# Attention: GpSimd pre-adds the sums of one step in nine (j = 4) in place of two (j = 2 and j = 6)

## The reference

```python
s = jnp.einsum('bqhgd,bkhd->bhgqk', qi, k)     # qi already scaled by Dh ** -0.5
p = jax.nn.softmax(s, axis=-1)
return jnp.einsum('bhgqk,bkhd->bqhgd', p, v)
```

## Time and profile before

| | |
|---|---|
| median of 3 runs | 3883.38 us (3882.13 to 3886.03) |
| the profiled execution | 3884.3 us |
| its span in the profile | 3882.8 us |
| attention stage | about 385 to 1220 us |
| TensorE / VectorE / ScalarE / GpSimd busy, whole span | 91% / 50% / 41% / 27% |

### The profile page before, as it was taken

One profiled execution on the slowest core, in us unless ns is written; L12 is line 12 of the kernel. 1 busy time (PEld: TensorE's weight loads), 2 busy tenths in 40 slices (PEclk: granted clock), 3 DMA queues, 4 the chain that ended last, 5 costly groups with the idle time before them and its releaser, 6 DMA issues. The chain is left out here.

```text
span 3882.8 us, 49412 instructions
## 1 busy us (share of the span) xinstructions
PE 3544.4 (91%) x17922; PEld 2928.6 (75%) x17922; DVE 1958.2 (50%) x2948; ACT 1583.5 (41%) x2216; POOL 1047.6 (27%) x606
## 2 busy tenths in 40 slices
PE   5886999999996999687869799999999999999998
PEld 2764777777775999466758588888888888888897
DVE  2775899999984111345833333343334333433354
ACT  2442888888885111573224422222222222222233
POOL 0553999999993000011201100000000000000000
PEclk8997999999997999667989899999999999999999
DMA  4332111111102221224545643343334333433374
GB/s 165 104 118 83 39 44 44 44 43 44 44 23 90 83 80 65 84 88 125 155 141 173 200 123 97 114 150 97 96 118 141 97 107 103 147 94 101 108 206 152
DMA packets 375237, 400.99 MB, mean 103 GB/s; under 512 B 37588, under 2 KB 282548, under 8 KB 375092
## 3 DMA queue, kind: packets, MB, share of 16 engines
q1 hardware_dynamic: 358888, 358.26, 29.6%
q0 software_dynamic: 8432, 31.46, 2.2%
q10 hardware_dynamic: 7776, 9.44, 0.7%
HBM read 318.02 MB, written 81.08 MB: 103 GB/s over the span
## 5 line engine op out<-in xcount | busy, mean ns | idle before, releaser
L798 POOL TENSOR_TENSOR att_tlo<-att_prob,att_thi 128x1024 fp32r<-128x1024 f32 x292 | 693.5, 2400 | 78.0 <-ACT att_thi L967 78.0
L1989 ACT ACTIVATE ff_whi<-ff_ws 128x2048 fp32r<-128x2048 f32 (+1 forms) x170 | 317.5, 1867 | 901.6 <-PE ff_p L333 883.9
L331 PE MATMUL ff_p<-ff_hhi,ff_whi 128*128 128x512 f32 (+1 forms) x1760 | 650.5, 370 | 35.5 <-DVE ff_hlo L2045 22.7
L332 PE MATMUL ff_p<-ff_hlo,ff_whi 128*128 128x512 f32 (+1 forms) x1760 | 649.5, 369 | 0.0
L333 PE MATMUL ff_p<-ff_hhi,ff_wlo 128*128 128x512 f32 (+1 forms) x1760 | 649.5, 369 | 0.0
L1993 DVE TENSOR_TENSOR ff_wlo<-ff_ws,ff_whi 128x2048 fp32r<-128x2048 f32 (+1 forms) x170 | 378.4, 2226 | 386.9 <-ACT ff_whi L1989 386.7
L1935 POOL TENSOR_TENSOR ff_rs<-ff_ms,neg_half 128x1 f32<-128x1 f32 x18 | 9.9, 552 | 1596.0 <-DVE ff_ms L2065 1596.0
L331 PEld LDWEIGHTS ff_p<-ff_hhi,ff_whi 128*128 128x128 f32 x1760 | 333.6, 190 | 93.1 <-issue 37.9
L962 ACT ACTIVATE att_prob<-att_p_s 128x512 f32<-128x512 f32 x584 | 341.1, 592 | 103.2 <-PE att_p_s L858 95.6
L333 PEld LDWEIGHTS ff_p<-ff_hhi,ff_wlo 128*128 128x128 f32 x1760 | 333.5, 189 | 55.5
L332 PEld LDWEIGHTS ff_p<-ff_hlo,ff_whi 128*128 128x128 f32 x1760 | 333.7, 190 | 54.8
(11 more groups left out here) (242 smaller groups left out, 6200.8 us busy)
## 6 DMA issues: line engine op xcount, KB each, us to landing
ff_ws<-in_w_ffn_dram SPq DMA_DIRECT2D x320, 512.0 KB, 4.7
att_aw<-in_ada_w_dram SPq DMA_DIRECT2D x8, 2048.0 KB, 8.4
proj_d<-gp_out SPq DMA_DIRECT2D x18, 784.0 KB, 4.0
hT_d<-qkv_hT SPq DMA_DIRECT2D x18, 512.0 KB, 2.8
qT_d<-qkv_qT SPq DMA_DIRECT2D x18, 512.0 KB, 2.8
att_qa<-qT_d SPq DMA_DIRECT2D x36, 256.0 KB, 2.8
gp_h<-hT_d SPq DMA_DIRECT2D x18, 512.0 KB, 4.9
qkT_d<-gs_qkT SPq DMA_DIRECT2D x18, 512.0 KB, 2.9
```

The source lines that it names most:

```text
L331: pe.matmul(out, ah, bh, start=first, stop=False)
L332: pe.matmul(out, ah, bl, start=False, stop=False)
L798: pool.tensor_tensor(tlo[:, sl, :], prob[:, sl, :], thi[:, sl, :].bitcast(F32), ALU.subtract).then_inc(s.lo, 1)
L1989: act.activation(whi[:, par, 0:cols], ws[:, par, 0:cols], ACT.Copy).then_inc(s.w_hi, 1)
```

## The change

One line: `FOLDED` names step 4 in place of steps 2 and 6. GpSimd's pre-adds of steps 2 and 6 go, and it pre-adds step 4. VectorE adds the two halves of steps 2 and 6 itself, and takes one pre-added tile for step 4. `ADDS` becomes 17 in place of 16, the buffer `fold` has one row in place of two.

```diff
     PLAN = [3, 2, 1, 2, 2, 3, 3, 0, 0]
     PLAN_FIRST = [3, 2, 1, 2, 2, 3, 3, 2, 0]
     AHEAD = 2
-    FOLDED = (2, 6)
+    FOLDED = (4,)
     BANKS = 3
     ADDS = 2 * NS - len(FOLDED)
```

## The result

The changed kernel takes 3890.4 us at the median (20 runs) against 3883.4 us for the kernel before (20 runs). The ratio is 1.0021, with a 95% interval of 1.0014 to 1.0028: slower by 8.2 us by the ratio and 7.0 by the medians, with 5.4 and 10.9 as the interval's ends. The profiled execution took 3894.1 us, with a span of 3892.6, 9.8 more than before. The two medians stand 7.0 apart, the two profiled executions 9.8; the difference between these is what single executions scatter by.

The account below looks back on a forecast made before the run. The prediction took a TensorE-VectorE loop over a ring of two maxima banks as the bound. Its terms, 15 x 0.53 + 15 x 0.12 - 0.5 - 0.9 = +8.4 us, gave a median of 3891.8 us, range 3883.5 to 3898.5.

Parts of the forecast that it names:

- Step 1: GpSimd in each latent unit: losing one pre-add of two, 1.29 us, gains nothing in units 1 to 30.
- Step 2: VectorE: one more add per unit; the one in kernel step 7 costs nothing, output product 0.12 late.
- Step 3: TensorE: a later reduce delays the 11th maxima product from 2.34 to 2.61, and the second exponential to 3.62.
- Step 4: Kernel step 5: VectorE idles 0.40 for GpSimd's pre-add, so TensorE issues the 15th product 0.53 later, at 6.95.
- Step 5: Rest of the unit: the 0.53 us stays in units with a chunk; units without one keep +0.12.
- Step 6: Ends of the stage: -0.5 us in unit 0 and -0.9 in the last latent unit, as waits for pre-adds go.
- Absorbed: Rival: existing waits or a shorter wait in kernel step 5 take the shift; 3882 to 3885 us, chance 0.23.
- No give-back: Rival: units without a chunk also keep 0.53; +14.5 us, 3897.9; chance 0.15 together with VectorE-bound.
- VectorE-bound: Rival: VectorE binds throughout, each extra add costs 0.60 in 31 units; +18.6 us, 3902; chance 0.15 shared with No give-back.
- GpSimd binds: Rival: each unit shortens by up to 1.25 us; 3845 us, or 3863 with half lost to VectorE; chance 0.08.
- The fold runs early enough: Rival: kernel step 4's exponentials don't move and VectorE comes later than 5.62; same time as Absorbed, no chance of its own.

Follow-up runs that it names:

- e3: The change with no pre-adds on GpSimd, so VectorE makes 18 adds per unit: 3883.2 us, ratio 1.0001 to the kernel before.
- e1: The change with GpSimd pre-adding step 2 alone in place of step 4: 3881.0 us, ratio 0.9994 to the kernel before.
- e2: The change with GpSimd pre-adding step 6 alone in place of step 4: 3883.8 us, ratio 1.0003 to the kernel before.
- e4: The change, with VectorE's first reduce in step 5 made before the pre-added sum: 3877.3 us, ratio 0.9984 to the kernel before.
- e9: GpSimd pre-adds steps 2 and 4, against 2 and 6 in the kernel before; VectorE still makes 16 adds: 3900.8 us, ratio 1.0047.
- e10: Pre-adds of steps 2 and 4 as in e9, plus step 5's first reduce before the pre-added sum: 3872.7 us, ratio 0.9971 to the kernel before.
- e7: The change with the modulation chunk's products behind step 6 in place of step 5: 3891.3 us, ratio 1.0019 to the kernel before.
- e8: The kernel before with the modulation chunk's products behind step 6 in place of step 5: 3890.1 us, ratio 1.0016.
- e6: The change with GpSimd pre-adding steps 2, 4 and 6 in place of 4 alone: 3904.5 us, ratio 1.0054 to the kernel before.
- e11: The change with the first reduce ahead of the add in steps 3 and 5: 3869.9 us, ratio 0.9966 to the kernel before.
- e5: The kernel before, with VectorE's first reduce in step 5 made before its two adds: 3883.6 us, ratio 0.9998.

## Why the prediction was right, and where it was not

*Step 1 (GpSimd's relief is worth nothing)* held. e3 takes all pre-adds away and no unit is shorter for it. The rule of the Trainium skill ("Perfetto Trace Analysis", Identifying the Most-Contended Engine) to optimise the engine with the highest busy share first failed here: GpSimd went from 96% to 90% of the stretch and the time rose. In e3 it went to 86% and the time stayed.

*Step 2 (the extra adds)* held to 0.01 us: the one in step 7 is free (e1), the one in step 3 moves the output product by 0.11 (2.47 for 2.48 predicted).

*Step 3 (a later reduce in step 3 holds TensorE)* held: the 11th product at 2.60 for 2.61, the exponential at 3.60 for 3.62. Alone it costs 0.10 to 0.12 per unit (e2, e3), so in units with a chunk it is a part of the 0.53 and the wait itself is the other 0.43.

*Step 4 (the new wait)* held in place and size: pre-add at 4.28 (4.29), add at 5.61 (5.62), reduce at 6.22 (6.22), 15th product at 6.95 (6.95). The waits sum to 10.2 us in 30 units (0.40 each predicted, 0.34 by the trace's count). GpSimd was free in front of the pre-add, as said. e4, e9 and e10 show that the loss is this wait with a reduce behind it: longer wait, larger loss; reduce moved ahead, no loss.

*Step 5 (what becomes of 0.53)* held: 0.53 in units with a chunk, 0.12 in the others; 9.7 us over 29 units and 9.8 with unit 30's own, where the sum had 9.75 over 30. e7 and e8 show the reason given for the difference. What the prediction didn't see is that step 3's late reduce alone gives the same 0.12 in units without a chunk (e2).

*Step 6 (the ends of the stage)* failed: predicted -0.5 and -0.9, measured 0.0 and +0.6. At the reciprocal of unit 1 the change is 0.11 late (423.14 against 423.03), but it entered the stage 0.10 late. From unit 30's reciprocal to the last one it takes 72.91 us against 72.24; 0.11 of these 0.67 are unit 30's own. In unit 0 the gain was there (the chunk's products began at 403.02 in place of 403.49), and was lost in step 7. Not all of it was the pre-add's: the granted clock is 0.78 and 0.88 from 395 to 400 and 400 to 405 us in the kernel before, and 1.00 in the change. Unit 0 has two maxima products there (`PLAN_FIRST`), so that VectorE's extra add stands between two reduces and not in front of an idle. VectorE's timeline of unit 0 in the change:

```profile
401.26 0.70 DVE L1037 TENSOR_TENSOR att_p_sum<-att_p_sum,att_fold 128x512 f32<-128x512 f32 x1 [1.47 <-POOL att_fold L796]
...
408.05 0.69 DVE L1037 TENSOR_TENSOR att_p_sum<-att_p_sum,att_prob 128x512 f32<-128x512 f32 x1
408.65 0.68 DVE L1013 TENSOR_REDUCE att_mx<-att_p_r 128x2 f32<-128x512 f32 x1
409.25 0.69 DVE L1037 TENSOR_TENSOR att_p_sum<-att_p_sum,att_prob 128x512 f32<-128x512 f32 x1
409.85 0.68 DVE L1013 TENSOR_REDUCE att_mx<-att_p_r 128x2 f32<-128x512 f32 x1
```

and in the kernel before:

```profile
408.54 0.69 DVE L1037 TENSOR_TENSOR att_p_sum<-att_p_sum,att_fold 128x512 f32<-128x512 f32 x1
409.14 1.29 DVE L1013 TENSOR_REDUCE att_mx<-att_p_r 128x2 f32<-128x512 f32 x2
```

Three instructions before, four after. I had taken the plan of the other units for unit 0 too.

In the last latent unit the VectorE wait of 3.7 us went, as predicted (one of 1.8 for the pre-add of step 4 came), but TensorE's clock fell at other places. Windows of the change (clock is the third number from the end), then of the kernel before at the same places of the unit:

```profile
1178.00:1188.00 10.00, 7.81 (x29) 6.33 (x29) 6.53 (x12) 7.69 (x13) 8.95 (x5) 0.83 0.04 14
1188.00:1196.00 8.00, 6.74 (x35) 5.20 (x35) 4.87 (x8) 7.16 (x11) 8.00 (x4) 1.00 0.15 49
...
1200.00:1210.00 10.00, 7.71 (x34) 6.02 (x32) 4.51 (x9) 6.85 (x12) 4.75 (x2) 0.83 0.00 0
```

```profile
1168.00:1178.00 10.00, 7.81 (x35) 6.24 (x35) 6.05 (x11) 8.90 (x15) 10.00 (x5) 1.00 0.04 13
1178.00:1186.00 8.00, 5.66 (x24) 4.39 (x23) 4.67 (x8) 5.50 (x9) 8.00 (x5) 0.80 0.14 49
...
1190.00:1200.00 10.00, 7.24 (x39) 5.68 (x37) 5.06 (x10) 8.17 (x14) 5.19 (x3) 1.00 0.01 2
```

TensorE idled 2.6 us for the spread reciprocals in both. In the change the granted clock is 0.83 in the mean of that stretch: a matmul of 512 columns takes 0.63 us up to 4.7 us after the unit's reciprocal, where it takes 0.39 in the kernel before, so this part ran at the lower level, 1.2 GHz. It makes ScalarE's second exponential of step 4 1.02 us later after the reciprocal than before (1182.65 - 1178.58 against 1171.73 - 1168.68).

That is not the loss at the end yet. The kernel before has such a stretch later, from 14.5 to 17.5 us after its reciprocal (0.80 in the mean of the window), and at VectorE's first copy of a context unit's sum (line 1034) that follows it the change is 0.99 us ahead (21.31 against 22.30 after the reciprocal). The predicted gain stood there, with the clock's part in it. Then the change has a second stretch at the lower level, from 25.8 to 28.4 (the window of 0.83 from 1200 us), where the kernel before has 1.00, and the next reciprocal comes at 31.80 against 31.23. So it is where these stretches fell that made the term positive.

That the same idle doesn't always end in a drop makes this term one that I could not have predicted from the rows; the range of -1.25 to 0 should have allowed for it. No experiment was made to settle when it drops, so this stays open, and so does the pre-add's own share of the term.

*The sum.* The terms of the steady units gave +9.75 and measured 9.8; the ends gave -1.4 and measured +0.6. At the stage's last reciprocal the profiled change is 10.5 us late, 0.1 of it brought along, and at the end of the span 9.8. The forecast of +8.4 lies within the measured interval of 5.4 to 10.9, and between the 7.0 of the medians and the 9.8 of the profiles. The steady term was right, and the ends were 2.0 too low in the one pair of executions that was profiled. That the forecast comes so near to the medians in spite of that is luck.

*The rivals.* "Absorbed" fell with the units' lengths. "No give-back" fell with the 0.12 of units without a chunk. "VectorE-bound" fell with e3, "GpSimd binds" with e3 and e6. "The fold runs early enough" fell with the add that waits 0.34 at 5.61.

## What to carry to other kernels

Handing work to another engine is priced by who stands behind the wait for it, not by the work: here a pre-add that saved VectorE 0.6 us made TensorE 0.5 us late, since a reduce that TensorE needed stood behind the wait. Moving that one reduce ahead turned the same hand-over from 0.21% slower into 0.16% faster (e4), and a second reduce moved in step 3 gave the fastest version (e11). Before you move work between engines, look for the instruction in an in-order queue that the critical engine waits for, and put it ahead of every wait on a third engine that it doesn't need. Relieving an engine that is busy for 96% of a stage gains nothing when nobody waits for its results.

## What the runs showed that I had not expected

Placing a reduce first is no gain by itself (e5: 0.23 shorter, 0.26 longer): it makes VectorE wait for TensorE, 0.15 to 0.21 us as the trace counts it, and only pays where VectorE has saved something in the same step. And the mean over two kinds of unit hides this: e5's 29 units are 721.7 us against 721.6, though neither kind of unit kept its time.

The same idle of TensorE, 2.6 us in the last latent unit, was followed by a lower clock at once in one execution (0.83 in the mean of the stretch) and not in the other (1.00). Each drop moves the end by about as much as the term itself: the change was 0.99 us ahead after the one drop of the kernel before, and 0.57 late after its own second one.

In units without a chunk the late reduce of step 3 alone (e2) and the same reduce together with the wait of step 5 (the change) give the same 24.59. Where two paths end this close together, an experiment on one of them alone seems to explain the whole.
